# Mixing A's two probability maps on TensorE, by diagonal matrices

## The reference, cut to what matters

```python
for s0 in range(0, seq, QBLOCK):
    e = s0 + QBLOCK
    s = jnp.einsum('bhmqd,bhmkd->bhmqk', q[:, :, :, s0:e], k[:, :, :, :e]) * scale
    p = _chunk_causal_softmax(s, s0)
    wts = p[:, :, 0] - lam * p[:, :, 1]
    outs.append(jnp.einsum('bhqk,bhkd->bhqd', wts, v[:, :, :e]))
```

## Time and profile before

| | us |
|---|---|
| median of three runs | 3924.4 |
| the profiled execution's own time | 3936.69 |
| span of its profile | 3934.9 |
| mean granted TensorE clock, of 2.4 GHz | 0.941 |
| A's first attention stage in the trace | 236 to 329 |
| A's second attention stage in the trace | 1280.4 to 1375 |

### The profile page before, as it was taken

One profiled execution on the slowest core, in us unless ns is written; L12 is line 12 of the kernel. 1 busy time (PEld: TensorE's weight loads), 2 busy tenths in 40 slices (PEclk: granted clock), 3 DMA queues, 4 the chain that ended last, 5 costly groups with the idle time before them and its releaser, 6 DMA issues. The chain is left out here.

```text
span 3934.9 us, 41674 instructions
## 1 busy us (share of the span) xinstructions
PE 3439.4 (87%) x16316; PEld 2628.2 (67%) x16316; DVE 1806.9 (46%) x2791; ACT 1207.1 (31%) x2125; POOL 63.2 (2%) x74
## 2 busy tenths in 40 slices
PE   7978897788799769896978989789999987989998
PEld 5856665624578543586967856668888844747886
DVE  4555695324363756684243459432222213423333
ACT  3243322333332612473212212232121121613222
POOL 0000000001000000000000002100000000000000
PEclk9998999989999889898989999899999998999999
DMA  3211211200221221592012121111111010022221
GB/s 136 86 47 51 85 43 43 91 22 5 86 84 58 52 98 64 207 357 77 32 43 86 43 81 68 43 64 64 65 64 65 32 64 22 1 76 88 94 96 64
DMA packets 47530, 290.19 MB, mean 74 GB/s; under 512 B 6903, under 2 KB 7159, under 8 KB 15960
## 3 DMA queue, kind: packets, MB, share of 16 engines
q1 hardware_dynamic: 46936, 286.63, 20.3%
q0 software_dynamic: 448, 1.57, 0.1%
HBM read 265.10 MB, written 14.68 MB: 71 GB/s over the span
## 5 line engine op out<-in xcount | busy, mean ns | idle before, releaser
L398 PE MATMUL bank<-high,slot_high 128*128 128x512 f32 x3280 | 1204.6, 367 | 146.2 <-DVE low L327 102.4
L399 PE MATMUL bank<-low,slot_high 128*128 128x512 f32 x3280 | 1195.1, 364 | 0.0
L400 PE MATMUL bank<-high,slot_low 128*128 128x512 f32 x3280 | 1187.5, 362 | 0.0
L378 DVE TENSOR_TENSOR slot_low<-slot,slot_high 128x2048 fp32r<-128x2048 f32 (+1 forms) x162 | 366.8, 2265 | 1154.7 <-ACT slot_high L372 1154.0
L398 PEld LDWEIGHTS bank<-high,slot_high 128*128 128x128 f32 x3280 | 623.8, 190 | 267.5 <-issue 145.4
L372 ACT ACTIVATE slot_high<-slot 128x2048 fp32r<-128x2048 f32 (+1 forms) x162 | 306.6, 1892 | 1327.9 <-PE bank L400 1104.7
L400 PEld LDWEIGHTS bank<-high,slot_low 128*128 128x128 f32 x3280 | 622.4, 190 | 100.5
L399 PEld LDWEIGHTS bank<-low,slot_high 128*128 128x128 f32 x3280 | 624.3, 190 | 95.6 <-issue 4.3
L802 DVE TENSOR_REDUCE peak<-bank 128x1 f32<-128x128 f32 (+2 forms) x224 | 109.7, 508 | 175.3 <-PE bank L923 75.0
L852 ACT ACTIVATE prob<-bank,peak_bias 128x128 f32<-128x128 f32 (+2 forms) x224 | 119.8, 540 | 108.0 <-DVE peak_bias L810 108.0
L435 PE MATMUL bank<-slot_high,high 128*128 128x256 f32 x448 | 128.1, 286 | 27.3 <-DVE low L325 27.3
(11 more groups left out here) (336 smaller groups left out, 4195.0 us busy)
## 6 DMA issues: line engine op xcount, KB each, us to landing
mod_raw<-in_mod SPq DMA_DIRECT2D x48, 1024.0 KB, 6.8
slot<-in_gu SPq DMA_DIRECT2D x44, 1024.0 KB, 4.8
slot<-in_a_in SPq DMA_DIRECT2D x32, 1024.0 KB, 4.8
slot<-in_e_rest SPq DMA_DIRECT2D x16, 1024.0 KB, 4.8
slot<-in_down SPq DMA_DIRECT2D x16, 1024.0 KB, 4.7
spectra<-f_spectrum SPq DMA_DIRECT2D x12, 1024.0 KB, 3.8
h_spectrum<-spectra SPq DMA_DIRECT2D x12, 1024.0 KB, 4.9
slot<-in_a_out SPq DMA_DIRECT2D x8, 1024.0 KB, 5.6
```

The lines of the kernel that those rows point to most:

```text
L378: dve.tensor_tensor(k.slot_low[s][:, 0:n], k.slot[s][:, 0:n], k.slot_high[s][:, 0:n].bitcast(F32), ALU.subtract).then_inc(k.low[s], 1)
L398: pe.matmul(out, wh, xh, start=kt == 0, stop=False)
L399: pe.matmul(out, wh, xl, start=False, stop=False)
L400: mm = pe.matmul(out, wl, xh, start=False, stop=kt == self.kt - 1)
```

## The change

VectorE no longer mixes the maps. It makes two diagonal matrices of 128 by 128 for each block, the identity scaled row by row by the first reciprocal and by minus lambda times the second. TensorE turns and mixes in one: for each tile of 128 keys it multiplies map 0's probabilities with the first diagonal and adds map 1's with the second, in the same place in PSUM. The transpose stays where there is one map. The buffers `mix` go, and four diagonals come; the semaphore `mix_step` counts one step for each block instead of two.

```diff
-        self.mix = [k.sb(f"mix{p}", most, ctx) for p in range(2)] if maps == 2 else [x[0] for x in self.prob]
+        self.diagonal = [[k.sb(f"diagonal{p}{m}", P, ctx) for m in range(2)] for p in range(2)] if maps == 2 else None
...
                 for c2 in range(0, n, P):
-                    mm = pe.transpose(k.ps[b][:, at + c2:at + c2 + P], self.mix[x % 2][:, c + c2:c + c2 + P], k.c("ident"))
+                    probs = [buf[:, c + c2:c + c2 + P] for buf in self.prob[x % 2]]
+                    if self.maps == 2:
+                        for m in range(2):
+                            mm = pe.matmul(k.ps[b][:, c2:c2 + P], probs[m], self.diagonal[x % 2][m][:, :],
+                                           start=m == 0, stop=m == 1)
+                    else:
+                        mm = pe.transpose(k.ps[b][:, at + c2:at + c2 + P], probs[0], k.c("ident"))
                 mm.then_inc(k.filled[b], 1)
...
-                dve.tensor_scalar(self.mix[x % 2][:, 0:n], self.prob[x % 2][0][:, 0:n], self.inv[:, first], None, ALU.mult)\
-                   .then_inc(chain.sem, 1)
-                dve.wait_ge(chain.sem, chain.at(2 * x + 2))
-                dve.scalar_tensor_tensor(self.mix[x % 2][:, 0:n], self.prob[x % 2][1][:, 0:n], self.inv[:, second],
-                                         self.mix[x % 2][:, 0:n], ALU.mult, ALU.add).then_inc(mixed.sem, 1)
+                dve.tensor_scalar(self.diagonal[x % 2][0][:, :], k.c("ident"), self.inv[:, first], None, ALU.mult)
+                dve.wait_ge(chain.sem, chain.at(x + 1))
+                dve.tensor_scalar(self.diagonal[x % 2][1][:, :], k.c("ident"), self.inv[:, second], None, ALU.mult)\
+                   .then_inc(mixed.sem, 1)
```

More of the change, by code:

```diff
@@ L815, in mix @@
                 dve.wait_ge(k.drained[b], u.full(b, x // 2))
-            n, first, second = self.keys_of(x), slice(2 * x, 2 * x + 1), slice(2 * x + 1, 2 * x + 2)
+            first, second = slice(2 * x, 2 * x + 1), slice(2 * x + 1, 2 * x + 2)
             if self.maps == 2:
@@ L891, in counts @@
         counts = dict(head_staged0=4 * self.staged_by, head_staged1=4 * self.staged_by, peaks_found=32, bias_ready=32, inverse_ready=32,
-                    probs_ready=32 if self.maps == 2 or self.wide else 0, mix_step=64 if self.maps == 2 else 32 if self.wide else 0,
+                    probs_ready=32 if self.maps == 2 or self.wide else 0, mix_step=32 if self.maps == 2 or self.wide else 0,
                     output_squared=32 if self.ssq is not None else 0, masks_in=16 * len(self.masks),
```

## The result

The changed kernel took 3946.99 us (median of four runs, 3939.04 to 3950.41), against 3925.03 for the kernel before: ratio 1.0055, 95% interval 1.0038 to 1.0073. The forecast was 3945.5.

A forecast was written before the change was run, and what follows sets the result against it. VectorE was taken to set the pace before (9.67 of 9.94 us), TensorE after. Periods of 11.70 us with ramp and tail gave +10.8 and +10.5 us a stage, +21.3 on 3924.4: 3945.5 us, range 3933 to 3957.

The forecast's parts named there:

- The price of T: TensorE's turning of a block's probabilities: four records a tile instead of one, 0.44 us a tile, not 0.11.
- O's records: TensorE's matmuls for a block's attention outputs: two float32 records a tile, pitch 0.11 us, 0.22 a tile.
- rival 5: TensorE's turning: an ordinary turn costs four transposes, 0.88 us a tile; 3997 us, chance 2%.
- The period: Four query blocks in A's attention: from 9.94 to 11.70 us, being 10.91 work, 0.67 waits, 0.12 start-ups.
- S(512): TensorE's scores of the 512-key block, 1.71 us from start to start; time 0 of the walked period.
- The clock: First period of each stage: mean granted clock 0.85 before; TensorE, fuller ahead of it, stays at 2.4 GHz.
- Ramp and tail: Before the first and after the last 384-key turning in each stage: -0.6 us and +0.4 us.
- So VectorE sets the pace now.: A's attention before the change: VectorE's chains fill 9.67 of 9.94 us, the 384-key mix handed over last.
- Rival 3: A's attention: TensorE hides the turning and VectorE sets the period, -11.4 us a stage; 3902 us, chance 2%.
- Rival 1: TensorE's waits in the period close up to 10.91 us, +10.5 us in all; 3935 us, chance 18%.
- Rivals 2: First period's half-clock stretch stays, with slower tail and longer waits: +4.4 us a stage at most; 3949 to 3954, chance 18%.
- Rival 4: Each diagonal pass on TensorE is one record: 0.22 us a tile, period about 9.75; 3921 us, chance 3%.

The follow-up runs named there:

- k4: Kernel before, VectorE mixing as before, but TensorE turns each tile of the mixed map by two ordinary matmuls against the identity; 3949.6 us, ratio 1.0066.
- k2: Changed kernel, but TensorE turns only map 0 by one transpose a tile, leaving map 1 and both scales out; 3920.4 us, ratio 0.9989 to before.
- k3: Changed kernel without TensorE's second matmul of each tile, so map 1 is missing; 3926.9 us, ratio 1.0004 to the kernel before.
- k1: The changed kernel measured again beside the kernel before; 3943.34 against 3925.01 us, ratio 1.0048.
- k9: k7 with ScalarE's factor 1/sum0 left out of its square and copy; 3925.4 us, ratio 0.9999 to the kernel before.
- k7: Kernel before with VectorE mixing in one fused instruction and ScalarE applying 1/sum0 to the outputs; 3931.7 us, ratio 1.0013.
- k5: Kernel before with two PSUM banks for A's outputs and a second scratch tile for ScalarE's squares; 3916.6 us, ratio 0.9977.
- k8: k7's single mixing instruction with k5's two output banks; 3905.44 us, ratio 0.9943 to the kernel before.
- k10: k2 with k5's two output banks, map 1 and the scales left out; 3901.6 us, ratio 0.9940 to the kernel before.
- k6: The changed kernel with k5's two output banks; 3938.16 us, ratio 1.0029 to the kernel before.

## Why the prediction was right, and where it was not

- **The price of T.** Predicted 0.44 us a tile, by the pitch of O's records. Measured 0.44 to 0.445, 640 records at 275 ns. The sentence of the Trainium skill that calls transpose mode four times faster for float32 ("TensorE: Matmul & The Clock Gate", Terms) would have made it 0.88 (rival 5); for a matmul of this form the trace says two records against one, at the same pitch. The Trainium skill's advice to use a transpose and not a standard matmul ("Perfetto Trace Analysis", Transposes) holds here: two ordinary matmuls a tile in place of the transpose cost 2.02 us a period (k4), one cost 0.46 (k2 to k3).
- **TensorE becomes the bound.** Right. It is busy 11.48 of 11.57 us (next fence; this counts each record to its modelled end, which covers most of the gaps; by starts it is 11.18 with the start-ups), and VectorE's busy time in a period is 7.02 us, against 8.66 in the earlier trace rows.
- **The period.** Predicted 11.70 with 0.35 and 0.29 us of waits at T(384) and O(256) and a small one at O(512). Measured 11.57: waits of 0.26 and 0.13, none at O(512); start-ups of 0.18, at T(384) and O(256), for 0.12; and 11.00 of work for 10.91. T(384) came 3.53 us after S(512), not 3.61. The waits are the mis-sized term (0.67 predicted, 0.39 measured). Seven periods are 0.9 us too long a stage, 1.8 of the 3 us by which +21.3 exceeds the +18.3 of k1; the rest is in ramp and tail. That 3945.5 lies only 1.5 us from the first median, 3946.99, is in part luck: that median was 3.6 us above the second.
- **The clock.** I took the half-clock stretch of the first period to go. It went: the first periods of both stages, from T(384) to T(384), run at a granted clock of 1.00, 2.4 GHz (the fence shows the first stage's). My reason for it is only half shown. The fall occurs in the first period in both stages of before and of k9 and in one of k7, whose other stage has it in its third period; all have one record a tile. In none with two or four does it occur; but k2, k5, k8 and k10, with one record and a shorter way to T(384) or two banks, don't have it either.

```profile
249.14:260.71 11.57, 11.48 (x77) 9.58 (x77) 7.02 (x29) 7.63 (x33) 0.00 (x0) 1.00 0.20 47
```

- **Ramp and tail.** Ramp -0.6 a stage predicted; -0.8 and -1.0 measured (8.98 and 8.37 us from first score to first T(384), before 9.81 and 9.33; in k1 it was -0.4 and -0.8). Tail +0.4 predicted; from the last T(384) to the end it took 6.56 us in both stages, before 6.48 and 7.03, so +0.1 and -0.5: the last outputs ran at the full clock (1.13 us, against 2.04 in the earlier trace rows).

```profile
330.14 1.60 PE L765 MATMUL bank<-diagonal,prob 128*128 128x128 f32 x12 [0.53 <-DVE diagonal L830]
...
335.57 1.13 PE L779 MATMUL bank<-a_value,turned 128*128 128x128 f32 x8 [0.72 <-ACT a_out L882]
```

- **"So VectorE sets the pace now."** Wrong, and it is the step to learn from. I summed VectorE's chains to 9.67 of 9.94 us, saw the largest wait (1.35 us before T(384)) released by the mix, and stopped. But just behind T(384) O(256) waited again, for `a_out` (0.20 us). The ring is S(512), its second maximum and bias, exp(512), the take of the 128-key block, O(256), and then 5.07 us round to S(512): 4.87 + 5.07 = 9.94 us, all from the earlier trace rows. In these 5.07 us lies a second take: T(128) is one record of 0.11 us, yet O(512) starts 0.32 us after it, 0.15 us behind the take of the 384-key block, which comes on ScalarE behind exp(256) and the evacuation of T(512). That is why two takes count in k7, whose trace names `a_out` before O(512). The mix is in neither half. In the kernel before, the two takes:

```profile
276.53 0.29 ACT L877 ACTIVATE a_out<-bank 128x128 f32<-128x128 f32 x1
...
282.38 0.28 ACT L877 ACTIVATE a_out<-bank 128x128 f32<-128x128 f32 x1
```

and the wait before O(512) in k7:

```profile
308.81 1.13 PE L773 MATMUL bank<-a_value,turned 128*128 128x128 f32 x8 [0.22 <-ACT a_out L875]
```

The forecast did not suffer, because its walk carried the take through the new period, and there TensorE's own work is the longer.
- **Rival 3** (faster, 3902) was built on the wrong pace: with TensorE at its old cost the steady period would have stayed at 9.93 (k2, 3920). Rival 1 (all waits close up) did not come, though k6 shows 0.20 us of it for a second bank. Rivals 2, 4 and 5 are refuted by the clock, the record count and the pitch. Rival 4's price was wrong as well: k3, with two records a tile, has 10.39 us and not about 9.75, since O(256) still starts 4.87 us after S(512).

## What to carry to other kernels

Before work is moved from a vector engine to TensorE inside a loop that is shared by three engines, add up TensorE's records over one period at their pitch: a float32 transpose that becomes two accumulated matmuls is four records for one, and here TensorE's work by that (11.0 us) exceeded the old period (9.94). The largest wait in a period does not name the bound; follow the ring until it closes and look at the wait after the largest: here the mix had a wait of 0.20 us for another engine behind it, and made shorter it gave back 0.01 us a period. Open the ring first (here one more PSUM bank, 0.31 us a period); then the shorter mix counts (0.51 us more in the full kernel k8, 0.85 in k10, which leaves map 1 out).

## What the runs showed of the hardware

A per-row factor read from SBUF lengthened ScalarE's square and copy of a 128x128 PSUM tile by 0.10 us each (279 to 376 ns, 288 to 383), which in k7 turned a saving into a loss. The Trainium skill has this price ("ScalarE: Activation LUTs", What ACT_TABLE_LOAD costs: some 93 ns for each per-partition operand), and the traces agree; I had left it out of what I expected of k7.

In these traces matmul records behind a wait start up more slowly than their pitch. T(384)'s twelve records take 1.44 us to the next record in k4 and k6, where at 0.111 us each they would take 1.33; T(512)'s sixteen, with no wait ahead, take 1.78, which is the pitch.

TensorE's clock can stand on an edge. k7 has the same instructions in both stages, and in both the clock fell from 2.4 to 1.2 GHz for some 3 us, but not at the same place. In the first stage it was the third period, in the second the first. Ahead of it PE had been busy 0.71 us of the 2 us from 270, and 0.55 of the 2 from 1298; but in the 2 us from 260 it was busy 0.55 as well, and no fall came. Windows from T(384) to T(384), the second and third period of the first stage and the first of the second:

```profile
260.95:271.25 10.30, 8.35 (x47) 5.97 (x47) 7.90 (x25) 8.32 (x33) 0.00 (x0) 1.00 0.23 53
271.25:282.74 11.49, 9.88 (x47) 7.31 (x47) 7.90 (x25) 8.35 (x33) 0.00 (x0) 0.85 0.20 46
...
1298.96:1310.45 11.49, 9.87 (x47) 7.41 (x47) 7.89 (x25) 8.35 (x33) 0.00 (x0) 0.85 0.19 43
```

What tips it was not tried.
